# Second attention of a two-block transformer kernel: the values of two steps multiplied together in every second step

## What is computed

```
q, k, v, u, y_branch, g_att, g_rec = jnp.split(z, SPLITS, axis=-1)
y_att = neighbourhood_attention(q, k, v, rpb[l]) @ w_att_o[l]

# in neighbourhood_attention
scores = jnp.einsum('bhrnqd,bhrnikd->bhrnqik', q_blk, kg).astype(jnp.float32)
scores = scores + bias[None]
scores = jnp.where(valid[:, :, None, :], scores, -1e30)
probs = jax.nn.softmax(scores, axis=(-2, -1)).astype(v.dtype)
out = jnp.einsum('bhrnqik,bhrnikd->bhrnqd', probs, vg)
```

## Time and profile before

| | us |
|---|---|
| median of 3 runs | 2827.86 (2826.81 to 2829.08) |
| the profiled execution | 2828.97 |
| its span on the core | 2827.2 |
| TensorE busy in it | 2801.3 (99%) |
| VectorE, ScalarE, GpSimd busy | 1726.0, 1333.7, 180.7 |

### The profile page before, as it was taken

How to read it: one execution, slowest core, us unless ns; L and a number is a source line. 1 busy time by engine, 2 the same in 40 slices (tenths; PEclk the granted TensorE clock), 3 DMA queues, 4 the chain that set the end, 5 groups by cost and what they waited for, 6 DMA issues and landing times.

```text
span 2827.2 us, 34929 instructions
## 1 busy us (share of the span) xinstructions
PE 2801.3 (99%) x13264; PEld 2270.1 (80%) x13264; DVE 1726.0 (61%) x2477; ACT 1333.7 (47%) x2149; POOL 180.7 (6%) x133
## 2 busy tenths in 40 slices
PE   8999999999999999999999999999999999999998
PEld 7777777888888888888777788888888888888886
DVE  5333356235866666678666524988235866666786
ACT  5444452114555454445355424887123655544452
POOL 1222420000000000000033200000000000000000
PEclk9999999999999999999999999999999999999998
DMA  3111111123344366532321111211113334384442
GB/s 127 38 31 38 39 38 51 52 62 117 131 149 153 150 236 231 186 109 93 128 61 53 45 54 59 60 54 59 53 60 142 134 149 156 139 322 162 156 134 71
DMA packets 86126, 302.75 MB, mean 107 GB/s; under 512 B 9552, under 2 KB 9680, under 8 KB 79696
## 3 DMA queue, kind: packets, MB, share of 16 engines
q1 hardware_dynamic: 84672, 295.88, 30.7%
q10 hardware_dynamic: 1296, 4.72, 0.6%
HBM read 225.07 MB, written 75.50 MB: 106 GB/s over the span
## 4 chain that ended last, share of the span: by engine, by line
PE 97%; DVE 1%; issue 1%; ACT 0%; DMA 0%; POOLq 0%; POOL 0%; SPq 0%; DVEq 0%; ACTq 0%
PE ps L404 24%; PE ps L2450 17%; PE pa L2756 11%; PE ps L2756 11%; PE ps L2785 9%; PE pa L2785 9%; PE pa L404 4%; PE ps L2803 3%; PE ps L2632 2%; PE pa L2560 2%; PE pa L2528 2%; PE pa L2539 1%; PE pa L2499 1%; PE pa L2632 0%; PE ps L2462 0%
## 5 line engine op out<-in xcount | busy, mean ns | idle before, releaser
L394 DVE TENSOR_TENSOR w_lo<-w_raw,w_hi 128x1024 fp32r<-128x1024 f32 x134 | 160.0, 1194 | 395.0 <-ACT w_hi L388 394.9
L388 ACT ACTIVATE w_hi<-w_raw 128x1024 fp32r<-128x1024 f32 x134 | 137.8, 1029 | 385.2 <-PE ps L404 265.7
L404 PE MATMUL ps<-a_hi,w_hi 128*128 128x512 f32 x896 | 276.5, 390 | 0.8 <-DVE a_lo L1756 0.8
L404 PE MATMUL ps<-a_hi,w_lo 128*128 128x512 f32 x896 | 275.9, 389 | 0.0
L404 PE MATMUL ps<-a_lo,w_hi 128*128 128x512 f32 x896 | 275.9, 389 | 0.0
L2450 PE MATMUL ps<-a_hi,w_hi 128*128 128x512 f32 x672 | 225.2, 416 | 9.2 <-DVE a_lo L1704 9.2
L1217 ACT ACTIVATE krh<-k_rraw 128x512 fp32r<-128x512 f32 x192 | 121.1, 631 | 229.8 <-PE ps L2785 118.0
L2450 PE MATMUL ps<-a_lo,w_hi 128*128 128x512 f32 x672 | 214.7, 401 | 0.0
L2450 PE MATMUL ps<-a_hi,w_lo 128*128 128x512 f32 x672 | 213.8, 399 | 0.0
L1984 DVE TENSOR_TENSOR krl<-k_rraw,krh 128x512 fp32r<-128x512 f32 x192 | 132.6, 691 | 132.3 <-ACT krh L1217 132.2
L404 PEld LDWEIGHTS ps<-a_hi,w_hi 128*128 128x128 f32 x896 | 167.7, 188 | 38.5 <-issue 2.5
(11 more groups left out here) (372 smaller groups left out, 6017.5 us busy)
## 6 DMA issues: line engine op xcount, KB each, us to landing
w_raw<-wstream SPq DMA_DIRECT2D x134, 512.0 KB, 3.5
k_rraw<-hff SPq DMA_DIRECT2D x224, 256.0 KB, 2.8
hff<-hbuf SPq DMA_DIRECT2D x32, 1024.0 KB, 3.9
wA<-wff SPq DMA_DIRECT2D x16, 2048.0 KB, 7.9
hff<-hbuf SPq DMA_DIRECT2D x32, 768.0 KB, 3.3
w_raw<-wff SPq DMA_DIRECT2D x32, 512.0 KB, 4.3
f_raw<-wff SPq DMA_DIRECT2D x32, 512.0 KB, 4.5
hres<-zt SPq DMA_DIRECT2D x16, 512.0 KB, 2.6
```

What stands on the lines that cost most here:

```text
L388: nc.scalar.activation(w_hi[:, slot, 0:n], w_raw[:, slot, 0:n], ACT.Copy).then_inc(s_whi, 1)
L394: nc.vector.tensor_tensor(w_lo[:, slot, 0:n], w_raw[:, slot, 0:n], w_hi[:, slot, 0:n].bitcast(F32), ALU.subtract).then_inc(s_wlo, 1)
L404: mm = nc.tensor.matmul(out[0:m, c], w[0:kp, slot, wofs:wofs + m], x[0:kp, k, c * HC:(c + 1) * HC], start=first and n == 0, stop=last and ...
```

## The change

In the second attention TensorE doesn't multiply values in even steps any more. In odd steps from 3 on it multiplies those of step s - 3 and right behind them those of step s - 2. So that the probabilities of two steps can stand side by side, there are four slots instead of two, and ScalarE's copy into a slot waits for the values of unit j - 4 instead of j - 2. The slots are four tensors now: two where `pt2` was, two from `Z0 + 6 KB` on. The last of these reaches 768 bytes beyond `T0`, and so `msk` moves up by 768 bytes and `bm` by 256. The first attention keeps its order.

```diff
-        msk = at("msk", [P, 6, 384], T0)
-        bm = at("bm", [P, 4, 384], T0 + 9 * KB + 512)
+        msk = at("msk", [P, 6, 384], T0 + 768)
+        bm = at("bm", [P, 4, 384], T0 + 9 * KB + 768)
-        pt2 = at("pt2", [P, 2, 384], G0 + 28 * KB)
+        pt2 = [at(f"pt2{n}", [P, 384], o_at) for n, o_at in enumerate((
+            G0 + 28 * KB, G0 + 29 * KB + 512, Z0 + 6 * KB, Z0 + 7 * KB + 512))]
...
+        def probs(b, j):
+
+            return pt1[:, j % 2] if b == 1 else pt2[j % 4][:]
...
                 def probs_out(j):
                     w = width(b, j)
                     act.wait_ge(s_T, j + 1)
-                    if j >= 2:
-                        act.wait_ge(s_pv, j - 1)
-                    nc.scalar.activation(pt[:, j % 2, 0:w], pa[:, 2, 0:w], ACT.Copy).then_inc(s_pt, 1)
+                    held = 2 if b == 1 else 4
+                    if j >= held:
+                        act.wait_ge(s_pv, j - held + 1)
+                    nc.scalar.activation(probs(b, j)[:, 0:w], pa[:, 2, 0:w], ACT.Copy).then_inc(s_pt, 1)
...
-                                                  pt[:, hh, a * P:(a + 1) * P], start=(a == 0), stop=(a == nb - 1))
+                                                  probs(b, j + hh)[:, a * P:(a + 1) * P], start=(a == 0), stop=(a == nb - 1))
...
-                    if s >= 2:
+                    if b == 1 and s >= 2:
+                        values(2 * (s - 2))
+                    if b == 2 and s >= 3 and s % 2:
+                        values(2 * (s - 3))
                         values(2 * (s - 2))
```

More of the change, by code:

```diff
@@ L764, in attention @@
                 vtok = vtok1 if b == 1 else vtok2
-                sm, pt = (sm1, pt1) if b == 1 else (sm2, pt2)
+                sm = sm1 if b == 1 else sm2
                 s_S, s_max, s_exp, s_T, s_pt, s_pv, s_oev, s_vt, s_vev = [sem(f"s_{x}{b}") for x in (
```

## The result

| | before | changed |
|---|---|---|
| median of 20 runs, us | 2827.9 | 2832.07 |
| lowest and highest | 2824.65 to 2829.69 | 2828.53 to 2834.16 |
| ratio, 95% interval | 1 | 1.0015 (1.0009 to 1.002) |
| span of the profiled execution | 2827.2 | 2832.0 |
| from the scores of step 2 to the first product of the next stage | 215.59 | 220.16 |

What follows compares the result with a forecast made beforehand. The prediction took TensorE's own queue to bound the kernel. Merging saves 2.5 us and nine new stalls cost 3.0, so +0.5 us on the median of 2827.86 gave 2828.4 us, range 2824.6 to 2831.2.

Steps and rivals of the forecast that it cites:

- What bounds the kernel: Second attention: TensorE's own queue sets the time, busy 99% of the span, with no block waiting in a normal step.
- What the merge saves: Values merged into odd steps: 0.15 us for each of 15 pairs, 0.25 in steps 32 and 33, together 2.5 us less.
- dearer end of 4.25: Rival on values' shape changes: the full 0.26 us saved for each of 16 blocks, 4.25 less; 2826.6 with stalls, chance 0.10.
- The stall of the second transposes: Nine even steps without a `v` batch: second transposes wait for the bank's copy until 4.25, 0.33 each, 3.0 us more.
- the row's own releaser: Step 1's 1.17 us idle: the row names VectorE's `sm`; the prediction took ScalarE's copy of the previous transposes instead.
- One sign: Profile after: TensorE idle 0.3 us before the second transposes in the nine even steps without a `v` batch.
- The six even steps with a batch of `v`: Steps 4, 6, 12, 14, 20, 22: second transposes at 4.33, free at 4.30, no stall; bounds 0 to 2.0 us, taken 0.
- copy of the probabilities at 3.71: Six even steps with a `v` batch: ScalarE's copy starts 3.71 us after the scores and ends at 4.20.
- all 15 even steps stall: Rival: the second transposes stall in every even step, 5.0 us more less 2.5, 2830.4 us; chance 0.15.
- VectorE falling behind: Rival: the short even step leaves VectorE busy when the next scores are in, additions start late, 2845.4 us; chance 0.03.
- What I had put at nothing: Four slots, moved `msk` and `bm`, second pair's values in odd steps, earlier `vtok` release, VectorE in shorter steps: no cost.
- The chances: Whole kernel: same within 0.2% 0.94, slower beyond it 0.04, faster beyond it 0.02.

Runs made afterwards that it cites:

- both_first: Changed kernel, in even steps ScalarE copies the first transposes ahead of the second exponential and any `v` batch ahead of the first; 2825.21 us, ratio 0.999.
- fill_21_15: Changed kernel with 21 projection matmuls in even steps (2 to 30) and 15 in odd ones instead of 18 and 18; 2830.3 us, ratio 1.0005.
- slots_only: Kernel before with only the four slots and moved tiles, each step's values still multiplied in their own step; 2828.09 us, ratio 0.9998.
- before_both: Kernel before, in even steps ScalarE copies the first transposes ahead of the second exponential and any `v` batch ahead of the first; 2828.19 us, ratio 0.9996.
- before_v_last: Kernel before, with ScalarE copying the batch of `v` behind the second exponential in all 12 steps that have one; 2838.78 us, ratio 1.0039.
- before_step1: Kernel before, with ScalarE copying the first transposes ahead of both exponentials in step 1 alone; 2826.35 us, ratio 0.9996.

## Why the prediction was wrong

**What bounds the kernel**: right. TensorE's own queue in this stage sets the time, and reading starts of blocks gave the nine even steps without a batch to 0.01 us (6.09 by the forecast, 6.08 or 6.09 measured).

**What the merge saves**: right in kind, a little small. 2.5 by the sum, 2.95 in both_first. Even steps there lose 0.78 to 0.85 where 0.81 was put, most of all steps 8, 16 and 24, whose first transposes come 2.20 or 2.21 after the scores instead of 3.05, and 0.62 to 0.66 came back for the twelve records, where 0.66 was put. Steps 32 and 33 together saved 0.38, not 0.25: from the last part of projection matmuls in step 31 to the first product behind step 33's values passes 9.20 us instead of 9.58. The first two projection matmuls behind a block of values take 0.57 (1624.62 to 1625.19), two that follow other projection matmuls 0.46 (1625.19 to 1625.65), and the sum had left this difference out. The dearer end of 4.25 is out. The rule of the Trainium skill ("TensorEngine Tiling (Array Packing)", Key Properties), by which each change of tiling mode drains TensorE, fits with this. With 17 changes fewer, 2.95 us were saved, 0.17 for each; that a drain is what they cost, no run shows by itself.

**The stall of the second transposes**: right, in place, cause and size. Nine steps, 4.25 forecast, 4.24 to 4.26 in all nine, and 3.0 us in all. The attribution against the row's own releaser held as well. One sign came out otherwise: 0.3 of idle time were to be seen, and TensorE's own rows show 0.15 in three of the nine steps and none in the others. It is the weight loads that show idle time in all nine, 0.54 to 0.56.

**The six even steps with a batch of `v`**: wrong, and this is the step that failed. The prediction says of the first transposes there, "these now come 0.81 sooner", and goes on to the second ones. It put bounds of 0 to 2.0 us on the six and took 0; they cost 4.5. The first transposes had a wait of their own: they write the bank from which ScalarE must first copy the batch of `v`, and ScalarE does this behind the first exponential. Both rows were in the trace of before, in step 4, with scores at 1435.35:

```profile
1438.77 0.49 PE L2539 MATMUL pa<-cst,sm 128*128 128x128 f32 x3
...
1437.98 0.58 ACT L860 ACTIVATE vtok<-pa 128x512 f32<-128x512 f32 x1
```

The copy ends at 1438.56 and the transposes start at 1438.77. As 0.14 passes from such an end to the transposes, 0.07 was to spare, and 0.81 was taken away: 0.74, six times 4.4. The order of the instructions, printed ahead of the prediction, even names the semaphore: `s_vev2`, which counts the copies of `v` out of the bank, stands among the waits of the transposes. I had asked who is late at the second transposes and not again at the first. With this term the sum would have been +4.9, against 4.57 in the stretch; the rest is for the most part the merge's gain, which the sum took 0.45 too small. The prediction's copy of the probabilities at 3.71 in these steps failed with the same term: the copy had to wait for the late transposes and starts at 3.90 or 3.91.

**The rivals**: that all 15 even steps stall was the nearest, with a time of 2830.4, but by the wrong mechanism, the second transposes, which in those six don't wait. VectorE falling behind did not happen in the changed kernel, and did in three steps of fill_21_15.

**What I had put at nothing**: right, by slots_only.

**The chances**: 0.94 for a change within 0.2% and 0.04 for slower beyond; it is 0.15%. The range failed at its upper end because the bounds of the unknown cost were taken from the stall that I knew.

## What to carry to other kernels

A block taken off the bound engine brings forward everything that comes behind it, so each wait behind it must be asked for its slack: not only the next but every one, and once for each kind of step. What was taken out here moved the rest up by 0.81 us; the slack behind it was 0.51 in one kind of step and 0.07 in the other. Where several producers share one bank, the copies that empty it belong at the front of the other engine's queue, ahead of work that nobody waits for yet: with two kinds of copies moved, the same change that cost 4.2 us gained 3. In the kernel before, where TensorE didn't wait for them, the same move was worth nothing (before_both).

A gap that repeats on the bound engine is read by the semaphores in the code, not by the releaser that a row names. The Trainium skill ("Perfetto Trace Analysis", Optimization Strategy) also sends the reader of a gap to the semaphores it waits on, to the instruction that updates them and to the source, and adds that gaps which repeat can mean too few buffers; here the buffers that were added were not the ones that lacked, and the one that lacked, the bank, wanted only to be emptied sooner.

## What the runs showed of the hardware that was not expected

- From the end of a copy on ScalarE in the records to the start of the transposes that waited for it, 0.10 us passed after the copy of probabilities (step 10 of the changed kernel, 4.15 to 4.25) and 0.14 to 0.15 after the longer copy of `v` (1436.72 to 1436.86 in before_v_last, 1494.01 to 1494.16 in the changed kernel). I had not expected two different values.
- In four kernels that do the same from step 2 on, before, slots_only, before_both and before_step1, the stretch took 215.59, 215.60, 215.57 and 215.40 us in one profiled execution each, while whole executions of the kernel before lie up to 5 apart. An effect of 1 us, 0.04% of the whole, can be settled in the stretch that it concerns.
- Two projection matmuls take 0.46 us to the next one's start where others stand ahead of them (1625.19 to 1625.65 in the kernel before), and 0.57 where they are the first ones behind values (1624.62 to 1625.19) or scores (1415.33 to 1415.90 in the changed kernel).
